# Adding the second operand of two weight sums onto the loaded tile in SBUF, in place of sums stored in HBM

## The chip, the cores and the metric

The kernel runs on one NeuronCore of one Trainium2 chip. The metric is the device time of one execution in microseconds (us); the median of three runs before the change is 1072.5 us. Names of engines: PE is the matrix engine, ACT the scalar engine, DVE the vector engine, POOL is GpSimd, SP the engine that here only issues transfers. All arithmetic is in 32-bit floats; PE takes each operand as a high and a low part, so one product is three matrix multiplications.

## What is computed

One block of an encoder on 512 tokens of width 1024: a gated feed-forward layer, a mixer of 8 + 8 attention heads, a second gated feed-forward layer, each with a normalised and modulated input and a gated addition to the residual, and a last normalisation.

```
h = modulate(x, g_ffn1, shift0, scale0)
x = x + 0.5 * gate0 * swiglu(h, w_ffn1_up, w_ffn1_down)
...                                   # the mixer
h = modulate(x, g_ffn2, shift2, scale2)
x = x + 0.5 * gate2 * swiglu(h, w_ffn2_up, w_ffn2_down)
return rmsnorm(x, g_final)

def swiglu(h, w_up, w_down):
    gate, up = split(h @ w_up, 2)     # w_up 1024 x 5632, w_down 2816 x 1024
    return (silu(gate) * up) @ w_down
```

The change concerns the last product, hidden (512 x 2816) times `w_ffn2_down` (2816 x 1024).

## The kernel before

The last product is made by a scheme of seven products in place of eight. The weight is cut in two halves of rows (1408 each) and two halves of columns (512 each), the hidden values likewise, and seven products P1 to P7 of a quarter of the weights (or a sum of quarters) with a quarter of the hidden values (or a sum of those) are made. They run in the order P1, P5, P2, P6, P7, P4, P3 (line 31). Each is made in four column tiles, so there are `N_DOWN` = 28 tiles or chunks, numbered t = 4 i + n: tiles 16 to 19 are P7, tiles 24 to 27 are P3. A tile of weights is 128 partitions x 11 x 128 floats, 704 KB, fetched in pieces of 512 bytes.

Three products (P1, P2, P4) use a plain quarter of the weights. Four (P5, P6, P7, P3) use sums: S1, S2 = first quarter + S1, S3, S4 = S2 + a quarter. All four sums are written to HBM ahead of time, in the tensor `d_sums`, by POOL's DMA queue: `DOWN_PIECES` (lines 67 to 69) lists 16 pieces of 1408 KB, each sum as two copies and two adding DMAs onto them. POOL issues them one after another (`down_piece`, line 769), each behind the one before: six during the first downward product, two at the start of the mixer, two later in it (lines 824 and 825), six during the second upward product (lines 827 to 829), each of these behind a count of finished products on PE (`w_used`). Between them stand 32 such pieces for the upward weights, and copies of the keys (`repeat_k`, line 713).

The way of one downward tile: SP issues its load (`load_down`, line 937) when the buffer is free, that is when the chunk that used it has ended; there are `D_RAW` = 6 buffers for loaded tiles. ACT rounds it into a high part (`down_high`, line 1536, the instruction is L1546), into one of `D_HI` = 5 buffers; DVE subtracts to get the low part in place of the loaded tile (`down_low`, L2087); PE's `down_chunk` (line 1464) waits for the low part. ACT and DVE handle tile t + 3 (`LEAD`) in their step t. Each engine works through a fixed order (lines 2026 to 2042 for ACT, 2787 to 2800 for DVE): in between stand the splits of the moving operand (L1573, L2120 and L2118), the evacuations of finished products (`keep_out`, L1555) and the additions of these to the residual (`add_out`, L2129).

At the end of these orders ACT has, in the step of tile 24, the evacuation of the last two parts of P4 and behind it `down_high(27)`; DVE has `down_low(27)` and behind it the last `add_out`. PE waits for this `add_out` before 16 transposes of the output (L1490) that stand between chunk 24 and chunk 25 (lines 1503 to 1506). After chunk 27 the last normalisation and the stores follow.

Of the kernel before, what the change touches and what calls it, by code (L numbers as in the profile page):

```python
# [5 lines left out]
ALU = mybir.AluOpType  # L6
ACT = mybir.ActivationFunctionType
F32 = mybir.dt.float32
# [5 lines left out]
P = 128  # L14
SEQ = 512
# [6 lines left out]
JOBS = 8  # L22
# [6 lines left out]
K_HALF = FC // 2  # L29
K_GROUPS = ((0, 4), (4, 8), (8, K_HALF))  # L30
P1, P5, P2, P6, P7, P4, P3 = range(7)
N_DOWN = 7 * 4
D_RAW, D_HI = 6, 5
LEAD = 3
HIGH_STEPS = ((0, 1), (2,), (), ())
LOW_STEPS = ((0, 1), (2,), (), ())
# [24 lines left out]
SEVEN0 = 2  # L61
T_DOWN2 = T_UP2 + 2 * SEVEN0 + 4 * (FC - SEVEN0)
HALF = SEQ // 2
N_PIECES = 8 * 4
N_EARLY, N_BEFORE = 6, 10
S2, S1, S3, S4 = range(4)
DOWN_PIECES = tuple((name, *source, half, add) for name, first, second in (
    (S1, (0, 1), (1, 1)), (S2, (0, 0), (S1, None)), (S3, (0, 0), (0, 1)), (S4, (1, 0), (S2, None)))
    for add, source in enumerate((first, second)) for half in range(2))
RAW = 4  # L70
SPLIT = 2
# [248 lines left out]
def hybrid_block_kernel(  # L320
# [4 lines left out]
    with ctx:  # L325
        def sem(name):
            return ctx.enter_context(nc.semaphore(name))
# [14 lines left out]
        def keep(name, shape, dt=F32):  # L342
# [32 lines left out]
        ssum_offset = top[0]  # L375
# [5 lines left out]
        region = top[0]  # L381
# [17 lines left out]
        KB = 1024  # L399
# [8 lines left out]
                  for q in range(4)] for s in range(3)]  # L408
# [7 lines left out]
        w5_lo = [at("w5_lo0", [P, WS], F32R, region + 40 * KB), at("w5_lo1", [P, WS], F32R, hid_offset + 20 * 2 * KB)]  # L416

        d_raw_at = [raw_offset + 14 * KB, raw_offset + 14 * KB + 5632, raw_offset, raw_offset + 5632,
                    region + 22 * KB, ssum_offset + 2 * 5632]
        d_raw = [at(f"d_raw{n}", [P, K_HALF, P], F32, place) for n, place in enumerate(d_raw_at)]  # L420
        d_lo = [at(f"d_lo{n}", [P, K_HALF, P], F32R, place) for n, place in enumerate(d_raw_at)]
        d_hi_at = [raw_offset + 14 * KB + 2 * 5632, region + 32 * KB, region + 32 * KB + 5632,
                   ssum_offset, ssum_offset + 5632]
        d_hi = [at(f"d_hi{n}", [P, K_HALF, P], F32R, place) for n, place in enumerate(d_hi_at)]
        assert split_offset == raw_offset + 16 * KB
        x_hi = [at(f"x_hi{n}", [P, K_HALF, HALF], F32R, region + (44, 0)[n] * KB) for n in range(2)]
# [47 lines left out]
        assert region + 2 * FC * SEQ * 4 + 3 * D * 4 <= beyond + 3 * SEQ * 4  # L474

        w_sums = nc.dram_tensor("w_sums", (4 * SEQ, (FC - SEVEN0) * P), F32).ap()
        d_sums = nc.dram_tensor("d_sums", (4, K_HALF * P, SEQ), F32).ap()

        bank = [ctx.enter_context(nc.psum_tensor(f"bank{i}", [P, SEQ], F32)) for i in range(8)]

# [1 line left out]
        wf_zero = sem("wf_zero")  # L482
        block_in = [[sem(f"block{p}_in{n}") for n in range(KC // 2)] for p in range(4)]
        piece_in, up_in = block_in, block_in[0:3]
        down_in = block_in[3] + [sem("down_in4"), sem("down_in5")]
        nat_sq, nat_ln, nat_rstd, xr_scaled = sem("nat_sq"), sem("nat_ln"), sem("nat_rstd"), sem("xr_scaled")
        xr_turned, xr_ready = sem("xr_turned"), sem("xr_ready")
        row_up, row_kept = sem("row_up"), sem("row_kept")
# [9 lines left out]
        w_hi_done, w_lo_done, w_used = sem("w_hi_done"), sem("w_lo_done"), sem("w_used")  # L498
# [8 lines left out]
            sem("silu_done"), sem("hid_f32"), sem("hid_hi_done"), sem("hid_done"))  # L507
        mix_zero, k_zero = sem("mix_zero"), sem("k_zero")
        scale_rest = sem("scale_rest")
        k_twice = [sem("k_twice0"), sem("k_twice1")]  # L510
        wf_split, wf_split_hi, f_logit, f_sum, f_act, f_dve = (
            sem("wf_split"), sem("wf_split_hi"), sem("f_logit"), sem("f_sum"), sem("f_act"), sem("f_dve"))
        chunk_hi, qk_ready, v_ready = (
# [20 lines left out]
        sums_made = sem("sums_made")  # L534
# [11 lines left out]
        down_v = [w.rearrange("o (k p) n -> (o p) k n", p=P) for w in (w_ffn1_down, w_ffn2_down)]  # L546
# [68 lines left out]
        def uses(f, q):  # L615

            return T_UP2 + 4 * (f - 1) + (2, 1, 3, 4)[q]
# [37 lines left out]
        def added(s):  # L655

            return 3 * KC + sum(len(parts) for _, parts, _ in SETS[:s]) + (s > 2)

        def last_added(n):

            return added(len(SETS)) + n
# [22 lines left out]
        def _(pool):  # L684
            g = nc.gpsimd
# [83 lines left out]
            def down_piece(name, k_half, c_half, half, add):  # L769

                pool.wait_ge(sums_made, 16 * pieces[0])
                rows = K_HALF * P // 2
                dst = d_sums[name, half * rows:(half + 1) * rows, :]
                if c_half is None:
                    src = d_sums[k_half, half * rows:(half + 1) * rows, :]
                else:
                    r0 = k_half * K_HALF * P + half * rows
                    src = down_rows[r0:r0 + rows, c_half * SEQ:(c_half + 1) * SEQ]
                if add:
                    ins = g.dma_start(dst, src, accum_op=ALU.add, max_dma_last_dim=2048)  # L780
                else:
                    ins = g.dma_start(dst, src)
                ins.then_inc(sums_made, 16)
                pieces[0] += 1
# [11 lines left out]
            for n, part in enumerate((v_hi[:, :, :, 1, :], v_lo[:, :, :, 1, :], pt_hi[:, :, ZERO_BLOCK, :],  # L796
# [4 lines left out]
                pool.wait_ge(mix_zero, n + 1)  # L801
                if n == 0:
                    repeat_k(0)
            for piece in DOWN_PIECES[N_EARLY:N_EARLY + 2]:
                down_piece(*piece)
            for j in range(1, JOBS):
                repeat_k(j)
                if j in (1, 2):
                    for r in (2 * j - 2, 2 * j - 1):
                        one_piece(sums_rows(S1, r), pieces_rows(up_b, r), True)  # L810
                    one_piece(sums_rows(S4, j + 1), pieces_rows(gate_b, j + 1), False)
                elif j == 3:
                    for r in range(3):
                        one_piece(sums_rows(S3, r), pieces_rows(up_a, r), True)
                elif j == 4:
                    one_piece(sums_rows(S3, 3), pieces_rows(up_a, 3), True)
                    one_piece(sums_rows(S2, 0), sums_rows(S1, 0), True)
                elif j == 5:
                    for r in range(1, 4):
                        one_piece(sums_rows(S2, r), sums_rows(S1, r), True)  # L820
                else:
                    for r in (2 * j - 12, 2 * j - 11):
                        one_piece(sums_rows(S4, r), sums_rows(S2, r), True)
                if j in (5, JOBS - 1):
                    down_piece(*DOWN_PIECES[N_EARLY + 2 + j // (JOBS - 1)])

            for n, piece in enumerate(DOWN_PIECES[N_BEFORE:]):
                pool.wait_ge(w_used, uses(SEVEN0 + 1 + 3 * n, 3))
                down_piece(*piece)


        @block.sync
        def _(sp):
# [54 lines left out]
            with sp.Fori(0, 2) as i:  # L888
                for j in range(4):
                    for part, (k0, nk) in enumerate(DOWN_PARTS):  # L890
                        t = T_DOWN1 + 3 * j + part
# [20 lines left out]
            def load_seven(f, q):  # L912

                n = f - SEVEN0
                if n == 0:
                    sp.wait_ge(w_used, T_UP2)
                elif n == 1:
                    sp.wait_ge(w_lo_done, T_UP2 + RAW)
                elif n == 2:
                    sp.wait_ge(w_used, T_UP2 + 4)  # L920
                else:
                    sp.wait_ge(w_used, uses(f - 3, q))
                if n == 0 and q == 1:
                    sp.wait_ge(sums_made, 16 * (N_PIECES + N_BEFORE))
                if q == 0:
                    src = up_v[1][:, :, f * P:(f + 1) * P]
                elif q == 3:
                    src = up_v[1][:, 4:KC, FFN + f * P:FFN + (f + 1) * P]
                else:
                    src = sums_v[:, KC * (q - 1):KC * q, n * P:(n + 1) * P]  # L930
                sp.dma_start(up_raw[n % 3][q][:].rearrange("p (k n) -> p k n", n=P), src).then_inc(up_in[n % 3][q], 16)
# [5 lines left out]
            def load_down(t):  # L937

                i, n = divmod(t, 4)
                if t < 2:  # L940
                    sp.wait_ge(w_used, uses(FC - 3, 3))
                elif t < 4:
                    sp.wait_ge(w_used, uses(FC - 1, (0, 2)[t - 2]))
                elif t < D_RAW:
                    sp.wait_ge(w_used, T_DOWN2)
                    sp.wait_ge(hid_f32, 2 * FC)
                else:
                    sp.wait_ge(w_used, T_DOWN2 + t - D_RAW + 1)
                if i in (P1, P2, P4):
                    k_half, c_half = {P1: (0, 0), P2: (1, 0), P4: (1, 1)}[i]  # L950
                    k = k_half * K_HALF
                    src = down_v[1][:, k:k + K_HALF, c_half * SEQ + n * P:c_half * SEQ + (n + 1) * P]
                else:
                    name = {P5: S1, P6: S2, P7: S3, P3: S4}[i]
                    if n == 0:
                        sp.wait_ge(sums_made, 16 * (N_PIECES + {S1: 4, S2: 8, S3: 12, S4: 16}[name]))
                    src = d_sums[name].rearrange("(k p) n -> p k n", p=P)[:, :, n * P:(n + 1) * P]
                sp.dma_start(d_raw[t % D_RAW][:], src).then_inc(down_in[t % D_RAW], 16)

            for t in range(N_DOWN):  # L960
# [560 lines left out]
        def _(act):  # L1521
# [13 lines left out]

            def down_high(t):

                act.wait_ge(down_in[t % D_RAW], 16 * (t // D_RAW + (2 if t % D_RAW < 4 else 1)))
                if t in (1, 2):
                    act.wait_ge(w_used, uses(FC - 1, 2 * t - 2))  # L1540
                elif t in (3, 4):
                    act.wait_ge(w_used, T_DOWN2)
                    act.wait_ge(hid_f32, 2 * FC)
                elif t >= D_HI:
                    act.wait_ge(w_used, T_DOWN2 + t - D_HI + 1)
                a(d_hi[t % D_HI][:], d_raw[t % D_RAW][:], ACT.Copy).then_inc(w_hi_done, 1)  # L1546
# [1311 lines left out]
```

## Time and profile before

| | us |
|---|---|
| median of the runs before (lowest, highest) | 1072.5 (1071.32, 1073.5) |
| profiled execution, its own time | 1071.11 |
| span in its profile, first to last instruction | 1069.2 |
| PE busy | 1051.9 (98%) |
| DVE busy | 718.0 (67%) |
| ACT busy | 533.8 (50%) |
| POOL busy | 57.1 (5%) |
| moved in all, mean rate | 223.08 MB, 209 GB/s |

The span is what the profile shows; the profiled execution's own time has 1.9 us more around it. Busy shares are of the span. A DMA has three times: when its engine issues it, when its data moves, and when it lands, which is when its semaphore is complete. Queue q1 holds the transfers that SP issues, q0 those that POOL issues. The share of the 16 DMA engines can be over 100%, since the times of packets overlap.

### The profile page before, as it was taken

The numbers are of one execution on the slowest core, as the hardware profiler recorded it, in microseconds if no ns is written. First come the engines' busy times: TensorE is split into PE (matmuls) and PEld (weight loads), VectorE is DVE, ScalarE is ACT, GpSimd is POOL, SyncE is SP. The second block draws the span as 40 slices with busy tenths as digits, with TensorE's granted clock in tenths as the row PEclk, the third lists the DMA queues.
The fourth block names the chain that finished last, engine by engine and source line by source line (L and its number), as shares of the span: only waits on it lengthen the run. The fifth ranks groups of instructions, "written<-read, shape, count | busy, mean of one in ns | idle before, by whom it ended". The sixth has DMA issues, their size and how long they took to land. (4 is left out here: it accounts for less than half of the span.)

```text
span 1069.2 us, 17031 instructions
## 1 busy us (share of the span) xinstructions
PE 1051.9 (98%) x6432; PEld 918.0 (86%) x6432; DVE 718.0 (67%) x1064; ACT 533.8 (50%) x871; POOL 57.1 (5%) x92
## 2 busy tenths in 40 slices
PE   8999999999999999999999999999999999999997
PEld 5788888888878889889878877889999999999996
DVE  5745555545554547886876676579866666699863
ACT  6422322322322225775887577448644544576653
POOL 1000000000000001211111011000000000000000
PEclk9999999999999999999999999999999999999999
DMA  9878888896599783799699967425999789867652
GB/s 341 253 230 281 265 277 289 271 306 181 157 297 229 197 258 112 138 224 207 156 193 183 203 162 160 131 79 144 238 233 234 223 251 242 197 185 198 180 163 79
DMA packets 250433, 223.08 MB, mean 209 GB/s; under 512 B 6924, under 2 KB 222588, under 8 KB 248316
## 3 DMA queue, kind: packets, MB, share of 16 engines
q1 hardware_dynamic: 233776, 154.45, 50.4%
q0 software_dynamic: 16128, 67.11, 25.9%
q8 instruction: 45, 0.74, 0.3%
q10 hardware_dynamic: 460, 0.58, 0.2%
q14 instruction: 24, 0.20, 0.1%
HBM read 217.93 MB, written 67.11 MB: 267 GB/s over the span
## 5 line engine op out<-in xcount | busy, mean ns | idle before, releaser
L982 PE MATMUL bank<-h_hi,w_hi 128*128 128x512 f32 (+1 forms) x592 | 230.5, 389 | 0.0
L983 PE MATMUL bank<-h_lo,w_hi 128*128 128x512 f32 (+1 forms) x592 | 223.5, 377 | 0.0
L984 PE MATMUL bank<-h_hi,w_lo 128*128 128x512 f32 (+1 forms) x592 | 223.5, 377 | 0.0
L2081 DVE TENSOR_TENSOR w_lo<-w_raw,w_hi 128x1024 fp32r<-128x1024 f32 x97 | 118.7, 1225 | 152.1 <-ACT w_hi L1534 151.5
L1534 ACT ACTIVATE w_hi<-w_raw 128x1024 fp32r<-128x1024 f32 x97 | 102.6, 1059 | 200.0 <-PE bank L984 192.6
L982 PEld LDWEIGHTS bank<-h_hi,w_hi 128*128 128x128 f32 x592 | 111.8, 189 | 24.5 <-issue 3.1
L983 PEld LDWEIGHTS bank<-h_lo,w_hi 128*128 128x128 f32 x592 | 111.7, 189 | 24.3 <-issue 3.1
L984 PEld LDWEIGHTS bank<-h_hi,w_lo 128*128 128x128 f32 x592 | 111.6, 189 | 22.6
L2241 DVE TENSOR_TENSOR up_lo<-up_raw,up_hi 128x1024 fp32r<-128x1024 f32 x80 | 86.6, 1086 | 21.1 <-ACT up_hi L1633 21.1
L984 PE MATMUL bank<-combo,up_lo 128*128 128x256 f32 x320 | 90.6, 283 | 0.0
L982 PE MATMUL bank<-combo,up_hi 128*128 128x256 f32 x320 | 90.5, 283 | 0.0
L983 PE MATMUL bank<-combo,up_hi 128*128 128x256 f32 x320 | 90.2, 282 | 0.0
L982 PE MATMUL bank<-x_hi,d_hi 128*128 128x256 f32 x308 | 87.2, 283 | 0.0
L984 PE MATMUL bank<-x_hi,d_lo 128*128 128x256 f32 x308 | 86.8, 282 | 0.0
L983 PE MATMUL bank<-x_lo,d_hi 128*128 128x256 f32 x308 | 86.6, 281 | 0.0
L1633 ACT ACTIVATE up_hi<-up_raw 128x1024 fp32r<-128x1024 f32 x80 | 75.3, 943 | 0.0
L982 PE MATMUL bank<-hid_hi,w_hi 128*128 128x512 f32 (+1 forms) x198 | 74.0, 374 | 0.1
L984 PE MATMUL bank<-hid_hi,w_lo 128*128 128x512 f32 (+1 forms) x198 | 73.5, 371 | 0.0
L983 PE MATMUL bank<-hid_lo,w_hi 128*128 128x512 f32 (+1 forms) x198 | 73.4, 371 | 0.0
L982 PE MATMUL bank<-h_hi,up_hi 128*128 128x256 f32 x240 | 68.0, 283 | 0.0
L983 PE MATMUL bank<-h_lo,up_hi 128*128 128x256 f32 x240 | 67.7, 282 | 0.0
L984 PE MATMUL bank<-h_hi,up_lo 128*128 128x256 f32 x240 | 67.6, 282 | 0.0
(293 smaller groups left out, 2268.4 us busy)
## 6 DMA issues: line engine op xcount, KB each, us to landing
w_sums<-in_w_ffn_up_dram POOLq DMA_DIRECT2D x24, 1280.0 KB, 8.6
ada_w<-in_w_ada_dram SPq DMA_DIRECT2D x56, 512.0 KB, 4.7
w_raw<-in_w_ffn_up_dram SPq DMA_DIRECT2D x48, 512.0 KB, 6.8
up_raw<-w_sums SPq DMA_DIRECT2D x40, 512.0 KB, 5.9
d_sums<-in_w_ffn_down_dram POOLq DMA_DIRECT2D x12, 1408.0 KB, 8.7
w_raw<-in_w_in_dram SPq DMA_DIRECT2D x28, 512.0 KB, 4.9
d_raw<-d_sums SPq DMA_DIRECT2D x16, 704.0 KB, 4.5
w_sums<-w_sums POOLq DMA_DIRECT2D x8, 1280.0 KB, 10.0
```

What stands on the lines that cost most here:

```text
L982: mm(dst, wh, xh, start=start, stop=False, skip_group_check=skip)
L983: mm(dst, wh, xl, start=False, stop=False, skip_group_check=skip)
L984: return mm(dst, wl, xh, start=False, stop=stop, skip_group_check=skip)
L1534: a(w_hi[:, s, :], w_raw[:, r, :], ACT.Copy).then_inc(w_hi_done, 1)
L1633: a(up_hi[f % 2][q][:], up_raw[n % 3][q][:], ACT.Copy).then_inc(w_hi_done, 1)
L2081: v.tensor_tensor(w_lo[:, s, :], w_raw[:, r, :], w_hi[:, s, :].bitcast(F32), ALU.subtract)\
L2241: v.tensor_tensor(up_lo[s][q][:], up_raw[s][q][:], up_hi[f % 2][q][:].bitcast(F32), ALU.subtract)\
```

## The change

`d_sums` keeps S1 and S2 only; `DOWN_PIECES` shrinks from 16 pieces to 8, all issued before or at the start of the mixer. For the eight tiles of P7 and P3 (`TWICE`) SP loads the first operand's quarter from `w_ffn2_down` itself, and POOL then issues an adding DMA of the second operand's quarter, from HBM onto the loaded tile in SBUF. POOL waits for the load's semaphore and, from the third on, for the addition two before; ACT's split waits for the addition's semaphore. There are seven buffers for loaded tiles and four for high parts: the seventh loaded tile takes the place of the fifth high part.

```diff
-D_RAW, D_HI = 6, 5
+D_RAW, D_HI = 7, 4
...
+TWICE = tuple(4 * i + n for i in (P7, P3) for n in range(4))
 DOWN_PIECES = tuple((name, *source, half, add) for name, first, second in (
-    (S1, (0, 1), (1, 1)), (S2, (0, 0), (S1, None)), (S3, (0, 0), (0, 1)), (S4, (1, 0), (S2, None)))
+    (S1, (0, 1), (1, 1)), (S2, (0, 0), (S1, None)))
...
+        def down_landed(t):
+            return 16 * (t // D_RAW + {4: 1, 5: 1, 6: 8}.get(t % D_RAW, 2))
+        def added_in(t):
+            n = TWICE.index(t)
+            return k_twice[n % 2], 16 * JOBS + 16 * (n // 2 + 1)
...
-                if j in (5, JOBS - 1):
-                    down_piece(*DOWN_PIECES[N_EARLY + 2 + j // (JOBS - 1)])
-
-            for n, piece in enumerate(DOWN_PIECES[N_BEFORE:]):
-                pool.wait_ge(w_used, uses(SEVEN0 + 1 + 3 * n, 3))
-                down_piece(*piece)
+
+            for n, t in enumerate(TWICE):
+                pool.wait_ge(down_in[t % D_RAW], down_landed(t))
+                if n >= 2:
+                    pool.wait_ge(*added_in(TWICE[n - 2]))
+                g.dma_start(d_raw[t % D_RAW][:], down_tile(t, (0, 1) if t // 4 == P7 else (1, 0)), accum_op=ALU.add)\
+                    .then_inc(added_in(t)[0], 16)
...
-                    sp.wait_ge(sums_made, 16 * (N_PIECES + N_BEFORE))
+                    sp.wait_ge(sums_made, 16 * (N_PIECES + len(DOWN_PIECES)))
...
-                if i in (P1, P2, P4):
...
+                if i in (P1, P2, P4, P7):
+                    src = down_tile(t, {P1: (0, 0), P2: (1, 0), P4: (1, 1), P7: (0, 0)}[i])
                 else:
...
-                    src = d_sums[name].rearrange("(k p) n -> p k n", p=P)[:, :, n * P:(n + 1) * P]
+                    src = d_sums[S1 if i == P5 else S2].rearrange("(k p) n -> p k n", p=P)[:, :, n * P:(n + 1) * P]
...
-                act.wait_ge(down_in[t % D_RAW], 16 * (t // D_RAW + (2 if t % D_RAW < 4 else 1)))
+                act.wait_ge(*(added_in(t) if t in TWICE else (down_in[t % D_RAW], down_landed(t))))
...
-                elif t in (3, 4):
+                elif t == 3:
```

P3's tile is loaded as S2 (from `d_sums`) and the quarter (1, 0) is added; P7's is the quarter (0, 0) and (0, 1) is added. Nothing changes in the work of PE, ACT and DVE.

## Rows read from the trace of the kernel before

**Rows 1.** The page: busy time of PE; its granted clock in 40 slices.
```profile
PE 1051.9 (98%) x6432; PEld 918.0 (86%) x6432; DVE 718.0 (67%) x1064; ACT 533.8 (50%) x871; POOL 57.1 (5%) x92
...
PEclk9999999999999999999999999999999999999999
```

**Rows 2.** Busy time by stretch (stretch: its us, busy us of each engine, clock, DMA).
```profile
20.00:780.00 760.00, 754.17 (x3991) 627.42 (x3990) 501.14 (x777) 366.56 (x607) 49.05 (x68) 1.00 0.77 209
...
1000.00:1069.20 69.20, 61.33 (x515) 60.68 (x513) 43.26 (x46) 33.05 (x60) 0.00 (x0) 0.98 0.44 134
```

**Rows 3.** Waits of PE, whole run: us in total, times, longest.
```profile
PE bank L1490 <- DVE xT L2129: 1.1, 1, 1.1
...
PE bank L1296 <- DMA k_hh_b<-k_hh_b: 0.5, 1, 0.5
...
PE bank L1296 <- DMA k_hh_a<-k_hh_a: 0.2, 1, 0.2
```

**Rows 4.** Timeline of SP: start, duration, tile load (here of tiles 15, 16, 24, 26).
```profile
986.72 0.36 SPq L958 DMA_DIRECT2D d_raw<-d_sums  x1
990.61 0.36 SPq L958 DMA_DIRECT2D d_raw<-d_sums  x1
...
1022.98 0.37 SPq L958 DMA_DIRECT2D d_raw<-d_sums  x1
...
1030.78 0.36 SPq L958 DMA_DIRECT2D d_raw<-d_sums  x1
```

**Rows 5.** Timeline of POOL: the last two stored additions.
```profile
887.61 1.15 POOL L780 DMA_DIRECT2D d_sums<-d_sums  x1 [29.38 <-PE bank L984]
917.69 1.13 POOL L780 DMA_DIRECT2D d_sums<-d_sums  x1 [28.93 <-PE bank L984]
```

**Rows 6.** Queues, 885 to 889 us: packets, MB, share; issues: KB, us to landing.
```profile
q1 hardware_dynamic: 2444, 1.24, 114.1%
...
d_sums<-d_sums POOLq DMA_DIRECT2D x1, 1408.0 KB, 12.6
up_raw<-w_sums SPq DMA_DIRECT2D x1, 512.0 KB, 4.8
```

**Rows 7.** Queues, 890 to 891 us.
```profile
q0 software_dynamic: 48, 0.10, 53.2%
```

**Rows 8.** Queues, 891 to 896 us; q1 has no row.
```profile
q0 software_dynamic: 485, 0.99, 111.0%
...
up_raw<-w_sums SPq DMA_DIRECT2D x2, 512.0 KB, 9.5
```

**Rows 9.** Timeline of ACT: high part of tile 4; last evacuation, high part of tile 27.
```profile
956.35 1.37 ACT L1546 ACTIVATE d_hi<-d_raw 128x1408 fp32r<-128x1408 f32 x1
...
1042.62 0.84 ACT L1555 ACTIVATE tmp_a<-bank,gate 128x256 f32<-128x256 f32 x2 [4.52 <-PE bank L984]
1043.35 1.38 ACT L1546 ACTIVATE d_hi<-d_raw 128x1408 fp32r<-128x1408 f32 x1
```

**Rows 10.** Queues, 975 to 1003 us: tile loads alone.
```profile
q1 hardware_dynamic: 9974, 5.05, 62.1%
...
d_raw<-d_sums SPq DMA_DIRECT2D x8, 704.0 KB, 4.5
```

**Rows 11.** Queues, 921 to 927 us (first row) and 594 to 600 us (second).
```profile
q0 software_dynamic: 597, 1.22, 111.1%
...
q0 software_dynamic: 235, 1.20, 104.3%
```

**Rows 12.** Timelines of DVE and PE: low part of tile 27, last addition, transposes.
```profile
1044.76 1.63 DVE L2087 TENSOR_TENSOR d_lo<-d_raw,d_hi 128x1408 fp32r<-128x1408 f32 x1 [4.74 <-ACT d_hi L1546]
1046.30 1.22 DVE L2129 TENSOR_TENSOR xT<-xT,tmp_a 128x1024 f32<-128x1024 f32 x1
...
1047.57 1.97 PE L1490 MATMUL bank<-ident,xT 128*128 128x128 f32 x16 [1.07 <-DVE xT L2129]
```

**Rows 13.** Busy time by stretch, 986.7 to 1043.3 us: DMA share is last but one.
```profile
986.70:1043.30 56.60, 56.60 (x478) 56.60 (x478) 43.91 (x35) 33.38 (x43) 0.00 (x0) 1.00 0.58 167
```

More of the change, by code:

```diff
@@ L64 @@
 N_PIECES = 8 * 4
-N_EARLY, N_BEFORE = 6, 10
+N_EARLY = 6
 S2, S1, S3, S4 = range(4)
+TWICE = tuple(4 * i + n for i in (P7, P3) for n in range(4))
 DOWN_PIECES = tuple((name, *source, half, add) for name, first, second in (
-    (S1, (0, 1), (1, 1)), (S2, (0, 0), (S1, None)), (S3, (0, 0), (0, 1)), (S4, (1, 0), (S2, None)))
+    (S1, (0, 1), (1, 1)), (S2, (0, 0), (S1, None)))
     for add, source in enumerate((first, second)) for half in range(2))
@@ L418, in hybrid_block_kernel @@
         d_raw_at = [raw_offset + 14 * KB, raw_offset + 14 * KB + 5632, raw_offset, raw_offset + 5632,
-                    region + 22 * KB, ssum_offset + 2 * 5632]
+                    region + 22 * KB, ssum_offset + 2 * 5632, ssum_offset + 5632]
         d_raw = [at(f"d_raw{n}", [P, K_HALF, P], F32, place) for n, place in enumerate(d_raw_at)]
@@ L422, in hybrid_block_kernel @@
         d_hi_at = [raw_offset + 14 * KB + 2 * 5632, region + 32 * KB, region + 32 * KB + 5632,
-                   ssum_offset, ssum_offset + 5632]
+                   ssum_offset]
         d_hi = [at(f"d_hi{n}", [P, K_HALF, P], F32R, place) for n, place in enumerate(d_hi_at)]
@@ L476, in hybrid_block_kernel @@
         w_sums = nc.dram_tensor("w_sums", (4 * SEQ, (FC - SEVEN0) * P), F32).ap()
-        d_sums = nc.dram_tensor("d_sums", (4, K_HALF * P, SEQ), F32).ap()
+        d_sums = nc.dram_tensor("d_sums", (2, K_HALF * P, SEQ), F32).ap()
         bank = [ctx.enter_context(nc.psum_tensor(f"bank{i}", [P, SEQ], F32)) for i in range(8)]
@@ L484, in hybrid_block_kernel @@
         piece_in, up_in = block_in, block_in[0:3]
-        down_in = block_in[3] + [sem("down_in4"), sem("down_in5")]
+        k_twice = [sem("k_twice0"), sem("k_twice1")]
+        down_in = block_in[3] + [sem("down_in4"), sem("down_in5"), up_in[2][0]]
         nat_sq, nat_ln, nat_rstd, xr_scaled = sem("nat_sq"), sem("nat_ln"), sem("nat_rstd"), sem("xr_scaled")
@@ L509, in hybrid_block_kernel @@
         scale_rest = sem("scale_rest")
-        k_twice = [sem("k_twice0"), sem("k_twice1")]
         wf_split, wf_split_hi, f_logit, f_sum, f_act, f_dve = (
@@ L657, in added, with down_tile @@
             return 3 * KC + sum(len(parts) for _, parts, _ in SETS[:s]) + (s > 2)
+        def down_tile(t, where):
+            k, n = where[0] * K_HALF, 4 * where[1] + t % 4
+            return down_v[1][:, k:k + K_HALF, n * P:(n + 1) * P]
+        def down_landed(t):
[3 more added lines that the diff above has]
+            return k_twice[n % 2], 16 * JOBS + 16 * (n // 2 + 1)
         def last_added(n):
@@ L803, in _ @@
                     repeat_k(0)
-            for piece in DOWN_PIECES[N_EARLY:N_EARLY + 2]:
+            for piece in DOWN_PIECES[N_EARLY:]:
                 down_piece(*piece)
@@ L948, in load_down @@
                     sp.wait_ge(w_used, T_DOWN2 + t - D_RAW + 1)
-                if i in (P1, P2, P4):
-                    k_half, c_half = {P1: (0, 0), P2: (1, 0), P4: (1, 1)}[i]
-                    k = k_half * K_HALF
-                    src = down_v[1][:, k:k + K_HALF, c_half * SEQ + n * P:c_half * SEQ + (n + 1) * P]
-                else:
-                    name = {P5: S1, P6: S2, P7: S3, P3: S4}[i]
-                    if n == 0:
-                        sp.wait_ge(sums_made, 16 * (N_PIECES + {S1: 4, S2: 8, S3: 12, S4: 16}[name]))
-                    src = d_sums[name].rearrange("(k p) n -> p k n", p=P)[:, :, n * P:(n + 1) * P]
+                if i in (P1, P2, P4, P7):
+                    src = down_tile(t, {P1: (0, 0), P2: (1, 0), P4: (1, 1), P7: (0, 0)}[i])
+                else:
+                    src = d_sums[S1 if i == P5 else S2].rearrange("(k p) n -> p k n", p=P)[:, :, n * P:(n + 1) * P]
                 sp.dma_start(d_raw[t % D_RAW][:], src).then_inc(down_in[t % D_RAW], 16)
```

## The prediction

> **What bounds the kernel now.** I read the page first: the matrix engine is busy 98% of the span at a granted clock of 0.9 or more in all 40 slices [rows 1], so there is no stage with another owner. The table by stretches says where the rest is: of 760 us in the middle 754.17 are busy, and the last 69.2 us have 7.9 us idle [rows 2]. The view of waits names what PE waited for: no line that ends at a DMA is over 0.5 us in the whole run, the two that touch this change's queue are 0.5 and 0.2 us and wait for copies of k, none waits for a sum of weights, and one wait stands in the tail, 1.1 us of the transposes (L1490) for the last big addition (L2129) [rows 3]. So neither the eight stored pieces that go (16 down to 8, all on POOL's queue) nor their traffic hold PE up today. The change can only win those crumbs; what it costs is to be read from the last 120 us, where the 28 downward chunks run, one each 3.9 us (tile loads are issued at 986.72 and 990.61, and those of tiles 24 and 26 at 1022.98 and 1030.78 us [rows 4]: each waits for a chunk's end).
>
> **Part 1, what is removed.** Eight stored pieces of 1408 KB. Two of them stand in POOL's order in the mixer, six between 767 and 918 us; the last two are the additions issued at 887.61 and 917.69 us [rows 5]. Loads of w_sums that fell into the first of these took 9.5 us [rows 8] in place of 4.8 [rows 6], yet PE did not wait. I count 0, with the ends 0 and -0.7 us (all waits on copies of k).
>
> **Part 2, seven raw and four high buffers.** Load t is issued when chunk t-7 ends, not t-6: 3.9 us earlier. ACT's split of tile t must now wait for chunk t-4, not t-5. ACT reaches it only in step t-3 of its order, behind steps that wait for the same or a later chunk (the split of tile 27 stands behind the evacuations that began at 1042.62, when chunk 23 had ended [rows 9]). Cost 0. Tile 6 comes from the start of the phase; the split of tile 4 ran at 956.35 [rows 9], after chunk 0. Cost 0, at most one landing's 4.5 us moved inside slack.
>
> **Part 3, the added work.** Eight tiles (16 to 19, 24 to 27) get, behind their load, an adding DMA of 704 KB from POOL into SBUF; ACT's split waits for it. First its three terms.
>
> Data time of a load: in 885 to 889 us, with loads alone and the engines full, 1.24 MB passed in 4 us, 309 GB/s [rows 6]; a tile is 0.721 MB, so 2.3 us. (Spread over an unsaturated stretch the same comes out: 62.1% of 28 us for 9974 packets [rows 10] is 2.46 us per 1408 packets.)
>
> Data time of an add: no row shows one into SBUF or in 512-byte pieces. Rows show adds in HBM: 597 packets, 1.22 MB in 6 us (2 KB each), and 235 packets, 1.20 MB in 6 us (5 KB each) [rows 11]. That is 161 and 408 ns per packet and engine, proportional to the bytes, 203 and 200 GB/s, so bytes count and packets hardly. By bytes an add of 0.721 MB takes 3.5 us. If an add is as two loads of 512-byte pieces, it is 4.6 us. I take 4.1. The far ends: 2.3 us (it costs as a load) and 88 packets per engine at 161 ns each, 14.2 us (a packet costs the same however small).
> The Trainium skill, Collectives: The Full Stack, section The bandwidth ceiling, says that a reducing transfer is slow because the add needs "two source reads", not because of the addition. The trace agrees: 203 GB/s for adds, 309 GB/s for loads. By that rule alone the add would be the 4.6 us end.
>
> Latency around the data: load, issue to landing 4.5 us alone [rows 10]. Add: issued 887.61 us [rows 5]; the window 890 to 891 us has 48 of its packets [rows 7] where a full one has 97 (485 in five [rows 8]), so its data begins near 890.5, about 2.8 us after the issue; it landed after 12.6 us [rows 6], at 900.2, of which 704 packets at 97 per us are 7.3 and the thinning out at the end about 1.0 to 1.5; I take 1.0 from the last data to landing.
>
> The DMA engines do one or the other: while that add ran, 891 to 896 us, the loads issued beside it moved nothing (485 packets of q0 and none of q1) and landed after 9.5 us [rows 8]. Whoever goes first, the work adds up. Now the sum. Load 16 is issued at 986.72 (where load 15 is today [rows 4]), lands 991.2; its add has data from 994.0; load 17 (990.61) is through by then. From here the engines have the ten loads 18 to 27 and eight adds to move before the add of tile 27 is done: 10 x 2.3 = 23.0 and 8 x 4.1 = 32.8. They run dry only once, for about 1.2 us, near 1042, when loads are over and add 26 is being issued. So add 27 lands at 994.0 + 23.0 + 32.8 + 1.2 + 1.0 = 1052.0 us.
>
> Is that late? Of the first group no. With adds ahead of loads the first two end at 998.1 and 1002.2; loads 18 and 19 follow up to 1006.8, load 18 lands at 1005.2 and its add's data begins 2.8 us later, at 1008.0; so the other two end at 1012.1 and 1016.2, each landing 1 us later. Then chunk 19 starts at 1022.98 (the issue of a load marks it [rows 4]), and before it ACT's 1.38 and DVE's 1.62 us are needed, so tile 19 must have landed by about 1019.9: 2.7 us to spare. For the second group loads 20 to 25 pass first (to about 1029), add 24 begins at 1030.0, and adds 24, 25, 26 land by about 1035, 1039, 1048, against chunks that start at 1042.5, after the transposes at 1047.57, and 3.9 us after that [rows 9, 12]: the three are in time.
> Tile 27 is late although its own chunk is the last. Behind its split (ACT, 1043.35 today) and its low half (DVE, 1044.76) stands, in DVE's order, the last big addition to the output (L2129, 1046.30 to 1047.5), and for that the transposes wait on PE (1047.57, with today's 1.07 us of waiting) and behind them chunks 25, 26, 27 [rows 9, 12]. That chain has no slack. ACT's split of tile 27 moves from 1043.35 to 1052.0, and everything behind it: **+8.7 us**. DVE's and ACT's work is unchanged in size.
>
> The sum against the profiled execution: it took 1071.11 us (span 1069.2 and 1.9 around it), so 1079.8. The median of the three runs is 1072.5, 1.4 above it; I forecast the median, 1072.5 + 8.7 = 1081.2 us. A difference of 0.2%, 2.1 us, is about what measurements of this kernel tell from none.
>
> **Rivals.**
> (a) The adds are cheap and all is hidden: not slower. For it: the second operand lies in SBUF, no row shows what reading it costs. If an add moves like a load (2.3 us), the total 994.0 + 23.0 + 18.4 + 1.0 = 1036.4 no longer rules, but load 27 does: issued 1030.78 [rows 4], landed by 1035.3, its add at least 2.8 + 2.3 + 1.0 later, 1041.4, before ACT reaches it at 1043.35. Time 1072.5. It decides at (1043.35 - 996.2 - 23.0)/8 = 3.0 us per add, 0.5 below the value by bytes; against it stand both sizes of add. Chance 0.15.
> The Trainium skill, DMA: Bandwidth & Descriptors, section Anatomy of one DMA, gives a fit of 2.0 us plus the bytes at 436 GB/s for a DMA issued by GpSimd; by it this add lands after an estimated 3.7 us and (a) is the outcome. The trace disagrees for adds: the fit makes 5.3 us of a piece of 1408 KB that took 12.6.
> (b) The first group stalls too: the two queues share the engines evenly instead of add first. Then each add takes about 8.2 us from 994.0 on, add 19 lands at 1026 or later, chunk 19 starts at 1029.1 in place of 1022.98, +6.1. The total of DMA work is the same, so add 27 still lands near 1052, and against a schedule that is 6.1 later the tail loses only 2.6 more: again about 1081, with the loss elsewhere. Against: loads stood still beside an add [rows 8]. Chance 0.12.
> (c) Small pieces are dear. At an intermediate 80 ns per packet (7.0 us an add) add 27 lands at 994.0 + 23.0 + 56.0 + 2.2 = 1075.2, +32, time 1104; at 161 ns it is 14.2 us each, 994.0 + 23.0 + 113.6 + 2.2 = 1132.8, +89, both groups stalled, time near 1162. Against it: no fixed part between 2 and 5 KB packets [rows 11]. For it: a quarter of the smallest size measured is an extrapolation, and POOL must write twice the packets per piece. Chance 0.11.
> (d) Faster: traffic that goes relieves something. It could give back the 0.7 us on k and no more, below what can be told. Chance of over 0.2%: 0.02.
>
> **Numbers.** Forecast 0.60, (a) 0.15, (b) 0.12, (c) 0.11, (d) 0.02. Faster 0.02, same 0.15, slower 0.83. The forecast's own range: adds of 3.5 us with loads of 2.1 give add 27 at 994.0 + 21.0 + 28.0 + 2.2 = 1045.2, +1.9; adds of 5.0 us give +15.9. The range goes on to (a) below and stops before most of (c): 1072 to 1094.
>
> **What would show it.** In the profile after: adds d_raw from the downward weights on POOL x8, 704 KB, landing in about 8 to 11 us; the stretch 986.7 to 1043.3 at 0.9 or more DMA share in place of 0.58 [rows 13]; loads that take 7 us or more; chunks 16 to 24 at today's times; then PE's wait at L1490 for L2129 grown from 1.1 to about 10 us, DVE's L2087 behind ACT's L1546 behind a DMA into d_raw. No wait of PE before that, in (b) a wait for DVE's d_lo near 1023. Wrong if ACT's last split still starts at 1043.4, or if the adds take under 3 or over 5.5 us of the engines each.

## The result, and the profile after

| | before | after |
|---|---|---|
| median of 4 runs, us | 1072.72 | 1087.21 |
| ratio, 95% interval | | 1.0144 (1.0132 to 1.0156) |
| profiled execution, its time / span | 1071.11 / 1069.2 | 1088.59 / 1086.8 |

A ratio, here and below, is the one estimated with its interval from the single runs; it is not the quotient of the two medians (1.0135 here) and can differ from it by 0.001.

The change costs 14.5 us where I forecast 8.7. The direction held and the time lies in the range; the size was off by a factor of 1.7. The view of waits of PE after, whole run (us in total, times, longest), names where:

```profile
PE bank L1501 <- DVE xT L2140: 9.3, 1, 9.3
...
PE bank L993 <- ACT tmp_a L1566: 2.1, 1, 2.1
...
PE bank L1307 <- DMA k_hh_b<-k_hh_b: 1.3, 1, 1.3
PE bank L993 <- DVE d_lo L2098: 0.9, 1, 0.9
...
PE bank L1307 <- DMA k_hh_a<-k_hh_a: 0.6, 1, 0.6
```

The first line answers to the 1.1 us of [rows 3]: the transposes (L1501 is L1490 of before) wait for DVE's last big addition to the output. The second and the fourth are new, and stand in the first group of additions, near 1020 and 1028 us: PE waits there for an evacuation of P6 by ACT, then for the low part of tile 19.

The timeline of POOL after shows the eight additions (here the first, the fourth, the fifth and the last: start, duration, idle before it and what ended it):

```profile
992.78 1.95 POOL L844 DMA_DIRECT2D d_raw<-in_w_ffn_down_dram  x1 [328.86 <-DMA d_raw<-in_w_ffn_down_dram]
...
1012.29 1.89 POOL L844 DMA_DIRECT2D d_raw<-in_w_ffn_down_dram  x1 [5.38 <-DMA d_raw<-in_w_ffn_down_dram]
1032.91 1.91 POOL L844 DMA_DIRECT2D d_raw<-in_w_ffn_down_dram  x1 [18.72 <-DMA d_raw<-d_sums]
...
1049.48 1.90 POOL L844 DMA_DIRECT2D d_raw<-in_w_ffn_down_dram  x1 [4.83 <-DMA d_raw<-d_sums]
```

The last is issued when load 27 has landed (load 27 had been issued at 1037.29 and took 11.9 us), and lands 8.5 us later: ACT's split of tile 27 starts at 1058.02. From there the timelines of ACT, DVE and PE are the chain of [rows 9, 12] again, each with what it waited for:

```profile
1058.02 1.38 ACT L1557 ACTIVATE d_hi<-d_raw 128x1408 fp32r<-128x1408 f32 x1 [1.84 <-DMA d_raw<-in_w_ffn_down_dram]
...
1059.43 1.63 DVE L2098 TENSOR_TENSOR d_lo<-d_raw,d_hi 128x1408 fp32r<-128x1408 f32 x1 [2.32 <-ACT d_hi L1557]
1060.97 1.22 DVE L2140 TENSOR_TENSOR xT<-xT,tmp_a 128x1024 f32<-128x1024 f32 x1
...
1062.24 3.67 PE L1501 MATMUL bank<-ident,xT 128*128 128x128 f32 x16 [9.29 <-DVE xT L2140]
```

The same 16 transposes took 1.97 us before [rows 12] and take 3.67 here. The busy times by stretch show why; the number behind POOL's is the granted clock, as a share of the full one:

```profile
1023.00:1026.00 3.00, 3.00 (x20) 3.00 (x19) 1.64 (x2) 0.02 (x1) 0.00 (x0) 0.65 1.12 301
...
1062.00:1068.00 6.00, 5.76 (x27) 5.76 (x28) 2.86 (x7) 3.31 (x12) 0.00 (x0) 0.50 0.04 17
```

After PE had stood still for 9.3 us its clock was at the lower of its two levels, half (1.2 in place of 2.4 GHz), for the next 6 us; after the 2.1 us wait it was at 0.65 in the mean of 3 us.

The sum over the two profiled executions, by when the same work starts. Load 16 is issued 1.36 us later than before (988.08 against 986.72 in [rows 4]). Load 26, issued when chunk 19 ends, comes at 1033.37, against 1026.90 for the load that this end set off before, 6.47 later: 1.36, the two waits of 2.13 and 0.95, and 2.03 left for the lower clock. The transposes start 14.67 later (1062.24 against 1047.57): 8.20 more, the grown wait. The end comes 17.6 later (1086.8 against 1069.2): 2.93 more, the clock again. So 17.6 = 1.36 early + 3.08 first group + 8.20 last addition + 4.96 clock. The early 1.36 us are mostly waits for copies of the keys (1.9 against 0.7 us), of which more below; this execution was itself 1.4 us above the median of its kernel, and the one before 1.6 below its own, which is why 17.6 stand here and 14.5 between the medians.

### The profile page after: what moved, and what is told of

Same layout as the page of the kernel before. It is cut to its first block and busy times, and to the rows that moved or that the text cites. A ratio compares the mean times of both kernels' runs of the same rounds, so it can differ in the third digit from the quotient of the medians.

```text
span 1086.8 us, 17029 instructions
## 1 busy us (share of the span) xinstructions
PE 1057.2 (97%) x6432; PEld 922.9 (85%) x6432; DVE 717.8 (66%) x1064; ACT 534.0 (49%) x871; POOL 65.5 (6%) x92
```

## The experiments

Theory A: the additions take time of the DMA engines and land late, and the order of ACT and DVE turns that into waits of PE. Each is compared with runs of the kernel before that were made beside it (medians 1071.6 to 1072.0 us).

**e1: the additions left out.**
```diff
-TWICE = tuple(4 * i + n for i in (P7, P3) for n in range(4))
+TWICE = ()
```


> The changed kernel with its eight additions in SBUF left out (the output lacks the second operand of P7 and P3); seven and four buffers, the removed stored pieces and all loads stay. Theory A (the loss of 14.5 us comes from the eight additions alone): the time of the kernel before, 1072.5 us, within 2. Theory B (a part lies in the buffers or in POOL's changed order, which the 1.3 us that the changed profile is late already at 955 us could be): 1073.8 or more, and the same 1.3 us at 955 us.

Measured: 1071.62 us, ratio 1.0004 (0.9994 to 1.0014). Everything is in the additions; the buffers, the removed pieces and POOL's new order cost and give nothing. The waits for copies of the keys were 0.6 us in this profile; in all profiles of this study together they lie between 0.6 (e4, with additions) and 1.9 us. I can't tie their scatter to the change.

**e2: plain copies in their place.**
```diff
-                g.dma_start(d_raw[t % D_RAW][:], down_tile(t, (0, 1) if t // 4 == P7 else (1, 0)), accum_op=ALU.add)\
+                g.dma_start(d_raw[t % D_RAW][:], down_tile(t, (0, 1) if t // 4 == P7 else (1, 0)))\
```


> The changed kernel with plain copies of the same 704 KB by the same queue, waits and places in place of the additions (the second operand overwrites the first). Theory A (time of the DMA engines: an addition takes 4.0 us of them, a plain copy 2.3): the last copy lands about 1044 to 1046 us, first group without a stall, time 1073 to 1077. Theory C (the serial chain load, POOL, issue, landing, with about 5 us of latency in each link, whatever the data): each copy still lands 8 us or more after its issue and the time stays at 1084 or more.

Measured: 1074.35 us, ratio 1.0030 (1.0017 to 1.0044). No wait in the first group, PE's wait at the transposes 2.7 us. So it is the addition's own cost, not the extra step through POOL: the same bytes, queue and waits cost 2.7 us as copies and 14.5 as additions. It is also what rival (a) of the prediction would have looked like, +2.7 and not 0. The theory written down beside it, that latency in each link costs the time whatever the data, asked for 8 us or more from issue to landing. That was nearly met (7.7 us median) without its consequence; the times tell them apart, the landing alone doesn't.

**e3 and e4: one group each.** The sum of the other product is stored ahead, with its four pieces where those of S3 had stood in POOL's order. For e3:
```diff
-TWICE = tuple(4 * i + n for i in (P7, P3) for n in range(4))
+TWICE = tuple(4 * i + n for i in (P7,) for n in range(4))
...
-    (S1, (0, 1), (1, 1)), (S2, (0, 0), (S1, None)))
+    (S1, (0, 1), (1, 1)), (S2, (0, 0), (S1, None)), (S4, (1, 0), (S2, None)))
```


> Additions in SBUF for P7's four tiles only; P3's sum is stored ahead as before. Theory A: the stall of the first group stays (3.0 us in the changed profile, and about 2.2 us of lower clock behind it), the 8.2 us at the last addition go: +5 us, 1077.5. If the two groups only hurt each other (loads of the second held back by the first): under +2.

> Additions in SBUF for P3's four tiles only; P7's sum is stored ahead as before. Theory A: from the first of them (data from about 1026 us) four additions of 4.0 and two loads of 2.3 us remain, the last lands near 1048 in place of 1058, and ACT needs it at 1043.4: +5 us and some clock behind a wait of PE of about 5 us, +6 to +8 in all, 1079 to 1080. If each link's latency is what counts (theory C): the last lands as late as now relative to its load, +12 or more.

Measured: P7 only 1076.64 us, ratio 1.0051 (1.0034 to 1.0068); P3 only 1080.85, ratio 1.0088 (1.0071 to 1.0106). The groups add up (0.51 + 0.88 = 1.39% beside 1.44% for both). e3 came out as expected, with two waits of 2.1 and 2.0 us in the first group. e4 was 1 to 2 us above what I expected: PE's wait was 7.7 us, not 5. Loads 26 and 27, issued at 1027.01 and 1030.92 beside the additions, took 8.0 and 10.7 us to land, and the last addition could be issued only behind load 27, at 1041.94; it landed at 1050.0. The row of PE's transposes in e4, again at half the clock:

```profile
1054.24 3.68 PE L1509 MATMUL bank<-ident,xT 128*128 128x128 f32 x16 [7.65 <-DVE xT L2148]
```

**e5: the order at the end turned.** ACT's last evacuations of P4 go before the split of tile 26, DVE's last big addition before the low parts of tiles 26 and 27.
```diff
-                    if n % 2 == 0 and (i or n):
+                    if n % 2 == 0 and (i or n) and (i, n) != (P3, 0):
...
+                    if (i, n) == (P4, 3):
+                        for m in range(2):
+                            keep_out(6, 2 + m)
...
+                    if (i, n) == (P4, 3):
+                        add_out(6, 0)
                     if 4 * i + n + LEAD < N_DOWN:
                         down_low(4 * i + n + LEAD)
...
-            add_out(6, 0)
```


> The changed kernel with the order at the end turned: ACT evacuates the last parts of P4 before the split of tile 26, DVE makes the last big addition to the output before the low parts of tiles 26 and 27. Theory A (the landing of the last addition costs only because the output's addition stands behind tile 27 in DVE's order): PE's wait of 9.3 us at the transposes goes, and with it the lower clock behind (2.9 us); chunks 26 and 27 wait 1 us or less: 1075 to 1077. Rival (the chunks themselves are late, tile 27's data is what PE lacks): the wait moves to chunks 26 and 27 and the time stays over 1082.

Measured: 1079.33 us, ratio 1.0064 (1.0049 to 1.0079). About half of the loss is gone by an order alone (7.9 us between the medians of the two changed kernels; 6.7 when each is taken against its own kernel before). The timelines of DVE and PE:

```profile
1051.75 1.22 DVE L2143 TENSOR_TENSOR xT<-xT,tmp_a 128x1024 f32<-128x1024 f32 x1
1055.06 1.63 DVE L2101 TENSOR_TENSOR d_lo<-d_raw,d_hi 128x1408 fp32r<-128x1408 f32 x1 [2.09 <-ACT d_hi L1557]
1059.00 1.62 DVE L2101 TENSOR_TENSOR d_lo<-d_raw,d_hi 128x1408 fp32r<-128x1408 f32 x1 [2.32 <-ACT d_hi L1557]
...
1053.03 1.97 PE L1501 MATMUL bank<-ident,xT 128*128 128x128 f32 x16 [0.45 <-DVE xT L2143]
```

Tile 27's low part is ready only at 1060.6, hardly earlier than before the turn, and PE waits 0.45 us at the transposes, which run at the full clock. I had expected 1075 to 1077; what is left is the first group's stall (4.3 us of waits in this profile) and 2.4 us at later transposes.

**e6: idle multiplications in the wait.** 36 multiplications whose result nobody reads, put before PE's wait, into a bank that is free there.
```diff
             down_chunk(P3, 0)
+            warm(36, 5)
             pe.wait_ge(x_upd, last_added(0))
```


> The changed kernel with 36 idle multiplications (128x512, some 7.7 us of PE) put into the wait of 9.3 us before the transposes, into a bank that is free there. Theory A (the last part of the loss is a lower granted clock after PE stood still: 0.50 from 1062 to 1068 us): the clock stays at 1.0, the end comes 2.5 to 3 us earlier, 1084.5. Rival (the slow stretch has another cause, such as transposes of data just written): the time stays at 1087 or goes up.

Measured: 1085.66 us, ratio 1.0128 (1.0114 to 1.0143). By the times alone this is not told apart from the change's 1.0144. The trace tells it: the clock in the stretch that had 0.50 is 1.00, and from the start of the transposes (1060.55) to the end of the span (1082.3) are 21.75 us, against 24.56 after and 21.63 before. That is 2.8 of the 2.9 us put down to the clock, shown. In this profile the first group's waits were 4.4 us, and the clock from 991 to 1044 us stayed at 1.00; so the 2 us of clock that the change's profile lost there don't come with every execution.

```profile
1062.00:1068.00 6.00, 6.00 (x53) 6.00 (x52) 4.12 (x7) 2.43 (x10) 0.00 (x0) 1.00 0.43 174
```

**e7: the kernel before, with DVE's last two turned.**
```diff
-            down_low(N_DOWN - 1)
             add_out(6, 0)
+            down_low(N_DOWN - 1)
```


> The kernel before with only DVE's order turned: the last big addition to the output before the low part of tile 27. Theory A: PE's 1.1 us of waiting before the transposes go, 1071.4, just at what can be told. Rival (the low part of tile 27, now 1.2 us later, or the wait for ACT holds something else up): 1072.5 or more.

Measured: 1070.77 us, ratio 0.9989 (0.9980 to 0.9997). PE's wait of 1.07 us before the 16 transposes is gone and nothing else took its place. It is the best version of this study: 0.11% below the kernel before, with the interval just clear of 1.

**e8: P3's additions with the turned order** (e4 and e5 together).

> Additions in SBUF for P3's four tiles only, with the turned order at the end. Theory A: nothing is late any more (no first group, no output's addition behind tile 27): 1071.5 to 1073, as the kernel before. Rival (late data as such): 1075 or more.

Measured: 1072.05 us, ratio 1.0000 (0.9992 to 1.0009). Of the 9.2 us of e4 nothing is left, with all four additions still in place: the late landing of tile 27 itself costs nothing.

**f1: as e3, and the loads of tiles 20 to 23 two chunks later.**
```diff
-                    sp.wait_ge(w_used, T_DOWN2 + t - D_RAW + 1)
+                    sp.wait_ge(w_used, T_DOWN2 + t - D_RAW + 1 + (2 if 20 <= t <= 23 else 0))
```


> As e3 (additions for P7's four tiles only), and the loads of tiles 20 to 23 are issued two chunks, 7.9 us, later. Theory D (the first group stalls because loads of later tiles, issued early by the seven buffers, share the DMA engines with the additions, 1:1 by packets): with them out of the way additions 18 and 19 land 5 us or more earlier, the two waits of PE near 1019 to 1025 (4.1 us in e3) go, 1072 to 1073.5. Rival (the chain of latencies load, POOL, addition sets the first group): the time stays at 1076.6, or the later loads make it worse.

Measured: 1073.36 us, ratio 1.0014 (1.0002 to 1.0026), against e3's 1.0051. PE's waits in the group fell from 4.1 to 1.3 us, the split of tile 19 starts at 1022.68 with load 16 issued about 2 us later than in e3, where it started at 1023.84: some 3 us earlier in its own schedule, where I had expected 5 or more. So it is mainly loads issued early that hold the additions back.

**f2: as e3, ACT's last evacuations of P6 before the split of tile 18.**
```diff
-                    if n % 2 == 0 and (i or n):
+                    if n % 2 == 0 and (i or n) and (i, n) != (P7, 0):
...
+                    if (i, n) == (P6, 3):
+                        for m in range(2):
+                            keep_out(4, 2 + m)
```


> As e3, with one change in ACT's order: the last evacuations of P6 come before the split of tile 18, behind which they stood. Theory D (the late landing of addition 19, about 1024 us, sets the stall; the evacuations only show it earlier): the wait on ACT (2.0 us) goes and the wait for the low part of tile 19 grows by as much, time within 1 us of e3's 1076.6. Rival (ACT's order makes the stall, as DVE's order did at the end): 2 us or more are gained, 1074.5 or less.

Measured: 1077.85 us, ratio 1.0053 (1.0035 to 1.0070). The wait on ACT went, the waits for low parts of tiles became 4.4 us; the time is 1.2 us above e3's, a little more than I allowed and the other way from the rival. Here the order is not what costs, unlike at the end: tile 19 itself is late.

**f3: all eight additions with e5's order and f1's later loads.**

> All eight additions, with the turned order at the end (e5) and the loads of tiles 20 to 23 later (f1). Theory D: nothing is late any more, 1072 to 1075. Rival: the stall of the first group stays, 1077 or more, e5 had 1079.3.

Measured: 1078.23 us, ratio 1.0056 (1.0039 to 1.0073), and I had expected 1075 or less. The first group's waits fell to 1.6 us, but the held-back loads now fell to the second group, whose additions came no earlier: its tile 25 is split only at 1049.25 and PE waits 2.5 us at the transposes, with the clock at 0.83 in the mean of 1050 to 1060 us. What f1 took out of the way of one group seems to stand in the way of the next; in these runs there was room for it only with P3's sum stored.

**f4: additions in long pieces.**
```diff
-                g.dma_start(d_raw[t % D_RAW][:], down_tile(t, (0, 1) if t // 4 == P7 else (1, 0)), accum_op=ALU.add)\
+                flat = w_ffn2_down.rearrange("o k n -> (o k n)")
+                part = flat[n * P * K_HALF * P:(n + 1) * P * K_HALF * P].rearrange("(p m) -> p m", p=P)
+                g.dma_start(d_raw[t % D_RAW][:].rearrange("p k n -> p (k n)"), part, accum_op=ALU.add)\
```


> The changed kernel with eight additions of the same 704 KB whose source is one contiguous row of 5632 bytes per partition (other numbers of the weights: the output is another) in place of 11 pieces of 512 bytes. Theory E (pieces of 512 bytes are what lets loads in 1:1 beside an addition and costs 182 in place of 200 GB/s; the sum I forecast held for long pieces): the additions go ahead of the loads as the stored ones did, take 3.6 us each, the first group has no wait of PE, addition 27 lands near 1047, time 1075 to 1079. Rival (the size of a piece is of no account): 1085 or more and the same two stalls.

Measured: 1082.95 us, ratio 1.0097 (1.0073 to 1.0121), between the two theories. The queues tell the halves apart. Rows of the change (first 1038 to 1041 us, where only addition 24 moves; then 1043 to 1047, where an addition and a load do), in packets, MB and share of 16 engines:

```profile
q0 software_dynamic: 1044, 0.53, 144.0%
...
q0 software_dynamic: 799, 0.41, 79.9%
q1 hardware_dynamic: 773, 0.40, 49.5%
```

and the same of f4 from 1002 to 1004 us, both queues moving:

```profile
q0 software_dynamic: 67, 0.38, 92.1%
q1 hardware_dynamic: 68, 0.03, 8.6%
```

In these stretches the two queues get equal numbers of packets, whatever their sizes: 799 to 773, and 67 to 68. So an addition in 512-byte pieces then gets half the packets, one in 5.6 KB pieces nearly all of the engines.

But this is not so in every stretch with work in both queues. In the first row above load 27 was waiting. Its issue, and its KB and us to landing:

```profile
1037.29 0.36 SPq L969 DMA_DIRECT2D d_raw<-d_sums  x1
...
d_raw<-d_sums SPq DMA_DIRECT2D x1, 704.0 KB, 11.9
```

It moved nothing until addition 24 was nearly through, near 1042, and had its half of the packets only beside addition 25. Load 18, issued at 995.97, stood still in the same way from 996 to 999 us beside addition 16 (1002 packets of q0, none of q1). No run here shows what decides between standing still and equal turns. As expected the first group had no wait of PE in f4. The end was worse, not better: PE waited 10.6 us at the transposes. Load 27, now the one pushed aside, landed at 1047.4, and only then could its addition be issued. That part of my expectation (addition 27 landing near 1047) was off by about 6 us. The additions of f4 take other numbers of the weights, so its output is another; the bytes moved are the same.

## Why the prediction was right, and where its size was off

- **What is removed, and the buffers: 0.** Right (e1). Nothing that stood on POOL's queue had held PE.
- **An addition takes 4.1 us of the engines.** Right: 1408 packets at 48 engine-us / 1044 = 46 ns over 16 engines are 4.05 us. Rival (c), that small pieces are dear, is out: in 5.6 KB pieces f4 moved 0.60 MB from 1033 to 1036 us, where the change moved 0.53 in as long.
- **The tail: +8.7 us by DVE's order.** Right in mechanism: PE's wait grew by 8.2, and e5, e7 and e8 show that the last addition to the output stands behind tile 27. That the size came so near is partly luck. With P3's additions alone (e4) the wait grew by 6.6 us, where I had expected about 5, and the four of P7 added only 1.6 more; in the sum from 994.0 they had counted for the rest, some 3.7.
- **"Of the first group no": the step that failed.** I had the additions go ahead of the loads and gave the group 2.7 us to spare. It stalled PE for 3.1 us, up to 4.4 in other profiles, and cost 5.0 us alone (e3). My ground was [rows 8], five microseconds with no packet of q1. But the loads I counted as waiting beside the addition had been issued only at 893.05 us and later; in the first two of those five there was nothing to hold back. After that the load did stand still (first packets of q1 between 896 and 897 us), so the reading held for some 3 of the five, and I took it for the rule. One microsecond of another stored addition, in the same trace of before, shows the turns. The queues of the kernel before from 807 to 808 us:

```profile
q0 software_dynamic: 83, 0.17, 90.3%
q1 hardware_dynamic: 86, 0.04, 21.7%
```

  That was rival (b), at 0.12: it had the place, the landing of addition 19 (1026 us; the split after it ran at 1025.98), a price of 6.1 us, and the cause in the main. f1 shows that cause: with the loads of tiles 20 to 23 later, 3.6 of e3's 5.0 us are gone. The landing was met partly by luck, since additions 16 and 24 did go ahead of the load issued beside them, as I had it, and (b) has all of them share.
  The Trainium skill, DMA: Bandwidth & Descriptors, section Queues, rings and completion order, says that each engine goes round-robin between the queues that have work, a packet at a time, where a packet is typically 9 to 17 descriptors. The runs agree on equal shares in some stretches (799 to 773, 67 to 68; the profile's packets here are single pieces of 512 bytes or 5.6 KB) and disagree in others (load 27 stood still for 4 us). By that rule (b) was the case to forecast.
- **"The total of DMA work is the same."** Only as long as the engines have work. When the first group stalled PE, loads 25 to 27 were issued up to 6.5 us later, and addition 27 landed at 1058.0, not 1052.0: the first group's loss did not come out of the tail's, as I had it in (b) (2.6 left), it came on top. e3 and e4 show the sum (5.0 and 9.2 us against 14.5).
- **The signs.** The wait at the transposes (9.3 us, about 10 named), the late loads (up to 17.9 us, 7 or more named) and the full DMA engines from 986.7 to 1043.3 us (1.10, 0.9 or more named) came as forecast. The additions landed after 8.2 to 13.7 us, not 8 to 11; chunks 16 to 24 were not at their old times, and PE did wait before the transposes, for a low part as (b) had it, and first for ACT.
- **The clock: missing.** 2.9 us at the end (e6), 2.0 in the first group in the profiled execution. I had priced each wait at its length.

## What to carry to other kernels

A transfer that is added to the critical phase is priced three times: its time on the shared DMA engines with everything else that is queued there, what stands behind its consumer in each engine's fixed order, and the clock that PE loses by standing still. The second can be had for nothing: of two instructions at the end of an order, the one that PE waits for goes first (7 to 8 us in the changed kernel, 1 us in the one before). To judge who goes first on the DMA engines, take several stretches in which both queues surely have issued work (one can show standing still and the next equal turns), and read packets, not bytes.

## What the runs showed of the hardware

- In several stretches in which POOL's and SP's queues both moved data they got equal numbers of packets (799 to 773 from 1043 to 1047 us in the changed kernel): with 5.6 KB against 512-byte packets one side got 0.38 MB and the other 0.03 in 2 us (f4). A load issued while an addition was under way first stood still: loads 18 and 27 in the changed kernel moved nothing for 3 to 4 us.
- An addition onto SBUF costs 46 ns per 512-byte packet and engine, 0.53 MB in 3 us or 178 GB/s in all, against 309 GB/s for loads [rows 6] and 200 to 203 for additions in HBM in longer pieces [rows 11].
- SP's issue of a load can itself be held: loads 22 and 23 in the changed kernel took 4.7 and 6.4 us to issue, where 0.4 is usual [rows 4], while transfers of both queues were under way.
- Waits of 7.7 and 9.3 us left PE at half its clock, the same 16 transposes taking 3.68 and 3.67 us, not 1.97; waits of 2 to 3 us lowered it in some profiles (0.65 over 3 us in the change) and not in others (1.00 in e6, with waits of 2.1 and 2.3 us).
